# Attention norm of a two-layer decoder step: root and reciprocal on six columns, spread back by TensorE inside the last gate tile

## The chip, the cores and the metric

The kernel runs on one NeuronCore of a Trainium2 chip. The core has TensorE (matrix products, called PE in the rows), VectorE (DVE), ScalarE (ACT), GpSimd (POOL) and SyncE (SP, which issues most loads). The metric is the device time of one execution in microseconds (us); lower is better. Three runs of the kernel before took 2000.6, 2001.98 and 2005.46 us, median 2001.98 us.

## The reference

512 prompt tokens and 32 sample tokens (8 sequences of 4) go through two layers. Each layer is a half SwiGLU, a mixer with two head groups, and another half SwiGLU. The mixer's softmax group has 8 query heads of 64 channels; its output `o_s` (544 tokens by 512 channels) is normalised over the channels of each token, and then goes with the output of the other group (gated linear attention, GLA) through one projection:

```python
def rmsnorm(x, g):
    y = xf * lax.rsqrt(jnp.mean(xf * xf, axis=-1, keepdims=True) + EPS)
    return (y * g.astype(jnp.float32)).astype(x.dtype)

o_s, k_keep, v_keep = swa_fn(qs, ks, vs, sinks)
o_s = rmsnorm(o_s, swa_g)
x = x + jnp.concatenate([o_g, o_s.astype(x.dtype)], axis=-1) @ w_out
x = x + 0.5 * swiglu(rmsnorm(x, n2), ffn2_gu, ffn2_down)
```

## The kernel before

Everything lies with channels on the 128 partitions and the 544 tokens along the free dimension, in two halves of 272. Weights come in chunks of 128x1024 (`w_raw`); ScalarE rounds a chunk to its high part (`w_hi`), GpSimd makes the low part (`w_lo`), and TensorE multiplies three products (high by high, low by high, high by low) for each of eight 128-row pieces. One such weight tile is 48 matmuls of 128x272. A PSUM "pair" is two banks that hold one 128x544 result.

The mixer is one list of steps (`mixer_steps`) that all engines walk through in the same order; each engine does its own part of a step, and semaphores join them. `JOBS` are the projection tiles in that order: job 19 is the gate tile `rG2`, job 20 is `squares` (no weight tile, only the norm's sum), job 21 is the last gate tile `rG3`, and jobs 22 to 29 are `out0` to `out7`, the half of the output projection that reads the normalised softmax output. Behind each job come the steps of its slot. What matters here:

- Slot 17, `ssq`: ScalarE squares the four 128-channel blocks of the attention output `qS`.
- Slot 18, `s_add`: VectorE adds the four blocks of squares into one, `sq_tile(0)` (lines 2274 and 2275).
- Job 20, `squares`: TensorE multiplies this tile by a 128x128 matrix of ones (line 943, two matmuls of 272 columns). Every partition of the pair then holds each token's sum.
- Slot 20: `s_norm` is a root on ScalarE over 128x544 (line 1611) and a reciprocal on VectorE over 128x544 (line 2278). `gs_kv 0` is a state update of the sample tokens, 16 small matmuls (line 1195) and an addition on VectorE (line 2266). `smix 0` and `smix 1` scale `qS` (line 2281); ScalarE then copies the high part (line 1623) and VectorE subtracts for the low part (line 2085).
- Slot 21, behind `rG3`: `att 3` (line 1134 on TensorE, line 2237 on VectorE), `smix 2`, `o 2` (lines 1149, 1155), `kv 6` and `kv 7` (line 1119 on TensorE, line 2222 on VectorE, tile `s_ring`), `smix 3`, and four SiLUs on ScalarE.
- Job 22, `out0`: 24 matmuls in four groups of six; group k waits until part k of the normalised output has its low part (`mix_ready`). It writes the PSUM pair that `squares` used.

In the feed-forward halves a norm over tokens is already done on six columns: `norm_sum` makes sums of one column for pieces of up to 128 tokens (`PIECES`: four of 128, two of 16), ScalarE and VectorE do root and reciprocal on 4 and 2 columns (lines 1285 and 1720), and `norm_spread` brings them to all partitions by six matmuls against the identity (line 797), in the middle of a weight tile.

Of the kernel before, what the change touches and what calls it, by code (L numbers as in the profile page):

```python
# [109 lines left out]


def job_pair(i):

    return 2 if i == 0 else 0 if i == 2 else i % 2
# [19 lines left out]
def mixer_steps():  # L134
# [35 lines left out]
            19: [("att", 2), ("o", 1), ("kv", 4), ("kv", 5)],  # L170
            20: [("s_norm", 0), ("gs_kv", 0), ("smix", 0), ("smix", 1)],
            21: [("att", 3), ("smix", 2), ("o", 2), ("kv", 6), ("kv", 7), ("smix", 3)] +
# [31 lines left out]
def trunk(nc, xT, stream, gains, lparams, wa2, cos_t, sin_t, swa_mask, samp_mask, gla_mask,  # L204
# [5 lines left out]
    def sb(name, shape, dt=F32, at=None):  # L210

        size = int(np.prod(shape[1:])) * 4
        if at is None:
            at = plan["at"]
            plan["at"] += -(-size // 64) * 64
        return nc.alloc_sbuf_tensor_at(name, list(shape), dt, offset=at)

    ctx = ExitStack()
    with ctx:
# [46 lines left out]
        bm = sb("bm", [P, 2])  # L266
        nrt = sb("nrt", [P, len(PIECES)])
        assert plan["at"] <= nc.sbuf_usable_end, plan["at"]
        LG, BG, GG, SG, SK, SKS, LG1 = 0, 24, 26, 30, 34, 42, 44
# [58 lines left out]
        def pair(i):  # L328
            return ps[:, 2 * i:2 * i + 2, 0:TH]

        def halves(ap):
            return ap.rearrange("p (h n) -> p h n", h=2)
# [72 lines left out]
        def sq_tile(j):  # L405
            return (g_buf, sq_buf)[j // 2][:, j % 2, :]

        def go_out():

            return ps[:, 6, 0:4 * SAMP].rearrange("p (h b g t) -> p h b g t", h=2, b=NB, g=2)  # L410
# [6 lines left out]
        def sem(name):  # L417
# [76 lines left out]
                   "ga_out", "go_done", "go_out", "klm_made", "fourfold", "s0_scaled", "gkv_done", "gkv_used", "r_silu",  # L494
                   "gsq", "gss_done", "g_root", "g_recip", "gbc_done", "ssq", "s_added", "ssum_done", "s_root", "q_paired",
                   "mix_made", "mix_high", "mix_ready", "kb_made"]
# [265 lines left out]
        def _(pe):  # L762
# [10 lines left out]

            def model_tile(dst, chunk, slot, h, stage=None, middle=None):

                pe.wait_ge(lo_ready, chunk + 1)
                for k in range(KT):
                    if stage is not None and k >= 5:
                        pe.wait_ge(*h_tile(stage, k))
                    if k == KT // 2 and middle is not None:  # L780
                        norm_spread(middle)
                    ins = product(dst, slot, k * P, h[:, 0, k, :], h[:, 1, k, :], k == 0, k == KT - 1)
                return ins
# [8 lines left out]
            def norm_spread(phase):  # L792

                pe.wait_ge(rs_ready, phase + 1)
                for c, (at, w) in enumerate(PIECES):
                    o = at % TH
                    ins = pe.matmul(ps[:, 6 + at // TH, o:o + w], nrt[0:w, c:c + 1].to_broadcast([w, P]),  # L797
                                    ident[0:w, 0:w], start=True, stop=True)
                ins.then_inc(rs_spread, 1)
# [139 lines left out]

            def square_sum(dst, squares):  # L940

                for hf in range(2):
                    ins = pe.matmul(dst[:, hf, :], ones[:, :], squares[:, hf * TH:(hf + 1) * TH],
                                    start=True, stop=True)
                return ins

            def mixer(l):
                ch = l * PL_LAYER + PL_MIX
                stage = l * 3 + 1
                for pos, (step, i) in enumerate(STEPS):  # L950
                    if step == "in":
# [3 lines left out]
                        if i >= 3:  # L955
                            pe.wait_ge(m["in_used"], i - 1)
                        dst = pair(job_pair(i))
                        if name == "squares":
                            pe.wait_ge(m["s_added"], 1)
                            ins = square_sum(dst, sq_tile(0))  # L960
                            ins.then_inc(m["ssum_done"], 1)
                            continue
                        if name[:3] == "out":
                            output_half(ch, 0, int(name[3]), dst)
                            continue
# [10 lines left out]
                        if name == "a":  # L976
                            for part in range(2):
                                pe.wait_ge(lo_ready, ch + (c + part + 1))
                                for k in range(4 * part, 4 * part + 4):
                                    ins = product(dst, (PL_MIX + c + part) % RING, (k % 4) * P, h_mid[:, 0, k, :],  # L980
                                                  h_mid[:, 1, k, :], k == 0, k == KT - 1)
                                if part == 0:
                                    ins.then_inc(chunk_done, 1)
                        else:
                            ins = model_tile(dst, ch + c, (PL_MIX + c) % RING, h_mid,
                                             stage if i == 0 else None, stage if i == 1 else None)
                        ins.then_inc(chunk_done, 1)
# [238 lines left out]
                for n in range(KT):  # L1226
                    if n == 2:
                        pe.wait_ge(m["in_used"], len(JOBS))
                    if n >= 4:
                        pe.wait_ge(*h_tile(l * 3 + 2, n - 4))  # L1230
                    output_half(ch, 1, n, pair((n + 2) % 4))
# [12 lines left out]
        def _(act):  # L1244
# [239 lines left out]
            def mixer(l):  # L1484
# [9 lines left out]
                for pos, (step, i) in enumerate(STEPS):  # L1494
# [108 lines left out]
                    elif step == "silu":  # L1603
                        act.wait_ge(m["in_used"], JOBS.index(f"rG{i}") + 1)
                        act.activation(rG[:, i, :], rG[:, i, :], ACT.Silu).then_inc(m["r_silu"], 1)
# [3 lines left out]
                    elif step == "s_norm":  # L1609
                        act.wait_ge(m["ssum_done"], 1)  # L1610
                        act.activation(halves(sq_tile(0)), pair(job_pair(JOBS.index("squares"))), ACT.Sqrt,
                                       bias=eps[:, :], scale=1.0 / (4 * P)).then_inc(m["s_root"], 1)
                    elif step == "gss":
# [77 lines left out]
        def _(dve):  # L1691
# [356 lines left out]
            def mixer(l):  # L2048
# [39 lines left out]
                for pos, (step, i) in enumerate(STEPS):  # L2088
# [182 lines left out]
                    elif step == "s_add":  # L2271
# [3 lines left out]
                        dve.tensor_tensor(sq_tile(0), sq_tile(0), sq_tile(3), ALU.add).then_inc(m["s_added"], 1)  # L2275
                    elif step == "s_norm":
                        dve.wait_ge(m["s_root"], 1)
                        dve.reciprocal(sq_tile(0), sq_tile(0)).then_inc(m["in_used"], 1)
                        dve.wait_ge(m["in_used"], JOBS.index("squares") + 1)
                    elif step == "smix":  # L2280
                        dve.scalar_tensor_tensor(out=qS[:, i, :], in0=qS[:, i, :],
                                                 scalar=lp[:, SG + i:SG + i + 1], in1=sq_tile(0),
                                                 op0=ALU.mult, op1=ALU.mult).then_inc(m["mix_made"], 1)
# [19 lines left out]

                dve.wait_ge(m["in_used"], len(JOBS))

# [160 lines left out]
```

## Time and profile before

| | us |
|---|---|
| median of three runs (lowest, highest) | 2001.98 (2000.6, 2005.46) |
| the profiled execution's own time | 1999.98 |
| its span, first to last instruction | 1998.2 |
| TensorE busy | 1951.4 (98%) |
| VectorE busy | 1350.1 (68%) |
| ScalarE busy | 1102.8 (55%) |
| GpSimd busy | 1094.3 (55%) |
| TensorE's mean granted clock, share of full | 0.988 |

The two mixers' stretches around the change are at 545 to 600 us (first layer) and 1525 to 1580 us (second layer) of the span. TensorE is busy nearly all the time, so a VectorE duration counts only where TensorE waits for it. A row of the chain shows which engine the end of the program hangs on at each moment; a row of the timeline gives the start, the duration and, in brackets, the idle time before it and what ended that. A matmul in plain fp32 stands as two records, so six matmuls are "x12".

### The profile page before, as it was taken

What the parts mean: (1) busy time and instruction counts of PE and PEld (TensorE: products, weight loads), DVE (VectorE), ACT (ScalarE), POOL (GpSimd) and SP (SyncE); (2) the same over time, 40 slices, a digit from 0 to 9 for tenths busy, and PEclk for the clock granted to TensorE, in tenths of its full rate; (3) what the DMA queues carried; (4) which work ended last, traced back from release to release, by engine and by line L of the source; (5) the groups of instructions that cost most, each with busy time, mean ns of one, the idle gap of its engine ahead of it and who ended that gap; (6) DMA issues with size and microseconds to landing.
All of it is one profiled execution on the core that took longest, in us unless ns stands there. A gap on an engine that the chain in (4) does not pass through costs nothing.

```text
span 1998.2 us, 40845 instructions
## 1 busy us (share of the span) xinstructions
PE 1951.4 (98%) x15562; PEld 1916.9 (96%) x15562; DVE 1350.1 (68%) x2450; ACT 1102.8 (55%) x2184; POOL 1094.3 (55%) x811
## 2 busy tenths in 40 slices
PE   5999999999999999999999999999999999999997
PEld 5999999998989999999999999999988899999997
DVE  7976687487245886578678757865764559766874
ACT  4664566536234565466656646663542356645662
POOL 3665566732215576566766656675222166755664
PEclk9999999999989999999999999999999999999998
DMA  3233232421211233233323333323121122332231
GB/s 136 82 108 108 85 101 91 150 85 45 94 59 64 78 106 106 93 99 101 99 81 101 101 101 101 105 88 138 64 95 47 67 80 91 100 108 91 96 107 65
DMA packets 92114, 185.65 MB, mean 93 GB/s; under 512 B 12880, under 2 KB 22768, under 8 KB 91376
## 3 DMA queue, kind: packets, MB, share of 16 engines
q1 hardware_dynamic: 84096, 170.04, 25.6%
q10 hardware_dynamic: 7824, 13.00, 1.9%
q8 instruction: 124, 2.03, 0.4%
q14 instruction: 70, 0.57, 0.1%
HBM read 178.09 MB, written 6.95 MB: 93 GB/s over the span
## 4 chain that ended last, share of the span: by engine, by line
PE 93%; DVE 5%; issue 1%; ACT 1%; DMA 0%; POOLq 0%; POOL 0%; DVEq 0%; ACTq 0%
PE ps L809 56%; PE ps L769 23%; PE ps L818 7%; PE ps L1038 1%; PE ps L1155 1%; PE ps L1027 1%; PE ps L1149 1%; PE ps L797 1%; PE ps L1208 1%; PE ps L1221 1%; PE ps L1010 0%; PE ps L1183 0%; DVE h_end L1703 0%; DVE h_end L1700 0%; PE ps L789 0%
## 5 line engine op out<-in xcount | busy, mean ns | idle before, releaser
L809 PE MATMUL ps<-rhs,w_hi 128*128 128x272 f32 x4256 | 805.0, 288 | 0.0
L809 PEld LDWEIGHTS ps<-rhs,w_hi 128*128 128x128 f32 x4256 | 669.6, 188 | 0.6 <-DVE ssum L1890 0.6
L809 PE MATMUL ps<-rhs,w_lo 128*128 128x272 f32 x2128 | 613.9, 288 | 0.0
L646 POOL TENSOR_TENSOR w_lo<-w_raw,w_hi 128x512 fp32r<-128x512 f32 x272 | 351.3, 1297 | 252.0 <-ACT w_hi L1308 252.0
L640 POOL TENSOR_TENSOR w_lo<-w_raw,w_hi 128x1024 fp32r<-128x1024 f32 x80 | 191.1, 2390 | 404.9 <-ACT w_hi L1252 390.4
L809 PEld LDWEIGHTS ps<-rhs,w_lo 128*128 128x128 f32 x2128 | 402.3, 189 | 0.0
L809 PE MATMUL ps<-act_c,w_hi 128*128 128x272 f32 x1792 | 354.5, 289 | 1.1 <-DVE h_mid L1741 0.8
L646 POOL TENSOR_TENSOR w_lo<-s_tmp,w_hi 128x512 fp32r<-128x512 f32 x216 | 283.1, 1323 | 32.6 <-ACT w_hi L1308 32.3
L809 PEld LDWEIGHTS ps<-act_c,w_hi 128*128 128x128 f32 x1792 | 287.7, 188 | 1.8 <-DVE h_mid L1741 1.2
L769 PE MATMUL ps<-h_mid,w_hi 128*128 128x272 f32 x1600 | 278.3, 292 | 0.0
L809 PE MATMUL ps<-act_c,w_lo 128*128 128x272 f32 x896 | 258.3, 288 | 0.0
L769 PEld LDWEIGHTS ps<-h_mid,w_hi 128*128 128x128 f32 x1600 | 229.4, 190 | 3.4 <-issue 2.8
L1308 ACT ACTIVATE w_hi<-ps 128x512 fp32r<-128x512 f32 x216 | 129.4, 599 | 182.1 <-DVE ps L1766 171.2
L1308 ACT ACTIVATE w_hi<-w_raw 128x512 fp32r<-128x512 f32 x272 | 172.1, 633 | 47.4 <-PE ps L809 40.3
L1308 ACT ACTIVATE w_hi<-s_tmp 128x512 fp32r<-128x512 f32 x216 | 136.7, 633 | 87.3 <-PE ps L809 86.0
L809 PEld LDWEIGHTS ps<-act_c,w_lo 128*128 128x128 f32 x896 | 169.3, 189 | 0.0
L769 PE MATMUL ps<-h_mid,w_lo 128*128 128x272 f32 x800 | 166.2, 289 | 0.0
L1766 DVE TENSOR_TENSOR s_tmp<-ps,w_raw 128x512 f32<-128x512 f32 x216 | 148.4, 687 | 17.4 <-POOL w_lo L646 3.1
L818 PE MATMUL ps<-act_p,pl_hi 128*128 128x272 f32 x768 | 159.5, 287 | 0.0
L1766 DVE TENSOR_TENSOR ps<-ps,w_raw 128x512 f32<-128x512 f32 x216 | 149.6, 692 | 2.7 <-ACT ps L1359 0.7
L1252 ACT ACTIVATE w_hi<-w_raw 128x1024 fp32r<-128x1024 f32 x76 | 80.2, 1058 | 127.9 <-PE ps L769 117.1
L1772 DVE TENSOR_TENSOR w_lo<-ps,w_hi 128x512 fp32r<-128x512 f32 x216 | 141.3, 683 | 1.2
(292 smaller groups left out, 3260.0 us busy)
## 6 DMA issues: line engine op xcount, KB each, us to landing
w_raw<-stream SPq DMA_DIRECT2D x380, 256.0 KB, 2.9
w_raw<-stream SPq DMA_DIRECT2D x80, 512.0 KB, 3.2
g_buf<-stream SPq DMA_DIRECT2D x52, 256.0 KB, 2.8
pl_raw<-stream SPq DMA_DIRECT2D x64, 192.0 KB, 2.8
x<-xT ACTq DMA_DIRECT2D x8, 272.0 KB, 5.7
y_d<-x SPq DMA_DIRECT2D x8, 272.0 KB, 2.1
s<-s_d ACTq DMA_DIRECT2D x2, 1024.0 KB, 4.9
s_s_d<-s ACTq DMA_DIRECT2D x2, 1024.0 KB, 3.9
```

Source lines behind the costliest of these rows:

```text
L640: pool.tensor_tensor(w_lo[:, p % RING, :], w_raw[:, p % RAW, :], w_hi[:, p % RING, :].bitcast(F32), ALU.subtract).then_inc(lo_ready, 1)
L646: pool.tensor_tensor(operand(w_lo, j, half), source(op, s, half), operand(w_hi, j, half).bitcast(F32), ALU.subtract).then_inc(pool_low, 1)
L769: ins = pe.matmul(dst[:, hf, :], w[:, slot, cols], r[:, hf * TH:(hf + 1) * TH], start=first and w is w_hi and r is rhs_hi, stop=last and r ...
L797: ins = pe.matmul(ps[:, 6 + at // TH, o:o + w], nrt[0:w, c:c + 1].to_broadcast([w, P]), ident[0:w, 0:w], start=True, stop=True)
L809: ins = pe.matmul(bank(s, at), w[:, k * P:(k + 1) * P], moving[:, k, side, r, :], start=fresh and k == 0 and w is hi and side == 0, stop=k ...
L818: ins = pe.matmul(bank(s, at), w[:, k * P:(k + 1) * P], act_p[:, k, side, hf * TH:(hf + 1) * TH], start=False, stop=k == PLAIN - 1 and sid ...
L1027: ins = pe.transpose(ps[:, 6 + a // 2, o:o + WIN], s_tile(i)[:, a * 256 + kb * WIN:a * 256 + (kb + 1) * WIN], ident[:, :])
L1038: ins = pe.matmul(ps[g * HD:(g + 1) * HD, 6, uu * WIN:(uu + 1) * WIN], vs_tok[:, b - 1 + kb, g * HD:(g + 1) * HD], p_t[:, o:o + WIN], star ...
L1252: act.activation(w_hi[:, p % RING, :], w_raw[:, p % RAW, :], ACT.Copy).then_inc(hi_ready, 1)
L1308: act.activation(operand(w_hi, j, half), source(op, s, half), ACT.Copy).then_inc(op_high, 1)
L1766: dve.tensor_tensor(source(name, s, half), first, second, ALU.add).then_inc(sum_made, 1)
L1772: dve.tensor_tensor(operand(w_lo, j, half), source(op, s, half), operand(w_hi, j, half).bitcast(F32), ALU.subtract).then_inc(dve_low, 1)
```

## The change

The sum over channels, the root and the reciprocal are done by tokens. `squares` on TensorE becomes six matmuls with one moving column: the stationary operand is a piece of the summed squares, and the result is one PSUM column per piece. ScalarE takes the root of 4 and 2 columns into a new small tile `sst`; VectorE takes the reciprocal there. TensorE spreads them to all partitions in six matmuls against the identity, placed in the middle of the weight tile `rG3`, into the same PSUM pair. The four `smix` steps read their factor from PSUM rather than from SBUF. The reciprocal's step moves behind `gs_kv 0` on VectorE, where VectorE then also waits for the spread. Since the pair is read until `smix 3`, `out0` on TensorE now waits for all four `smix` steps. The summed squares no longer count as an evacuated job (`evacuated`).

```diff
+def evacuated(i):
+    return i - (i > JOBS.index("squares"))
-            20: [("s_norm", 0), ("gs_kv", 0), ("smix", 0), ("smix", 1)],
+            20: [("s_norm", 0), ("gs_kv", 0), ("s_recip", 0), ("smix", 0), ("smix", 1)],
+        sst = sb("sst", [P, len(PIECES)])
+        def squares():
+            return pair(job_pair(JOBS.index("squares")))
...
+                    if k == KT // 2 and inside is not None:
+                        inside()
...
-            def square_sum(dst, squares):
-                for hf in range(2):
-                    ins = pe.matmul(dst[:, hf, :], ones[:, :], squares[:, hf * TH:(hf + 1) * TH],
-                                    start=True, stop=True)
-                return ins
+            def square_spread():
+                pe.wait_ge(m["s_recip"], 2)
+                for c, (at, w) in enumerate(PIECES):
+                    ins = pe.matmul(squares()[:, at // TH, at % TH:at % TH + w], sst[0:w, c:c + 1].to_broadcast([w, P]),
+                                    ident[0:w, 0:w], start=True, stop=True)
+                ins.then_inc(m["s_spread"], 1)
...
-                            ins = square_sum(dst, sq_tile(0))
+                            for c, (at, w) in enumerate(PIECES):
+                                ins = pe.matmul(dst[0:w, 0, c:c + 1], sq_tile(0)[:, at:at + w], ones[:, 0:1],
+                                                start=True, stop=True)
...
                         if name[:3] == "out":
+                            if name == "out0":
+                                pe.wait_ge(m["mix_made"], 4)
...
-                                             stage if i == 0 else None, stage if i == 1 else None)
+                                             stage if i == 0 else None, stage if i == 1 else None,
+                                             square_spread if name == "rG3" else None)
...
-                        act.activation(halves(sq_tile(0)), pair(job_pair(JOBS.index("squares"))), ACT.Sqrt,
-                                       bias=eps[:, :], scale=1.0 / (4 * P)).then_inc(m["s_root"], 1)
+                        w = PIECES[-1][1]
+                        act.activation(sst[:, 0:4], squares()[:, 0, 0:4], ACT.Sqrt, bias=eps[:, :],
+                                       scale=1.0 / (4 * P)).then_inc(m["s_root"], 1)
+                        act.activation(sst[0:w, 4:6], squares()[0:w, 0, 4:6], ACT.Sqrt, bias=eps[0:w, :],
+                                       scale=1.0 / (4 * P)).then_inc(m["s_root"], 1)
...
-                    elif step == "s_norm":
-                        dve.wait_ge(m["s_root"], 1)
-                        dve.reciprocal(sq_tile(0), sq_tile(0)).then_inc(m["in_used"], 1)
-                        dve.wait_ge(m["in_used"], JOBS.index("squares") + 1)
+                    elif step == "s_recip":
+                        dve.wait_ge(m["s_root"], 2)
+                        w = PIECES[-1][1]
+                        dve.reciprocal(sst[:, 0:4], sst[:, 0:4]).then_inc(m["s_recip"], 1)
+                        dve.reciprocal(sst[0:w, 4:6], sst[0:w, 4:6]).then_inc(m["s_recip"], 1)
+                        dve.wait_ge(m["s_spread"], 1)
                     elif step == "smix":
-                        dve.scalar_tensor_tensor(out=qS[:, i, :], in0=qS[:, i, :],
-                                                 scalar=lp[:, SG + i:SG + i + 1], in1=sq_tile(0),
+                        dve.scalar_tensor_tensor(out=halves(qS[:, i, :]), in0=halves(qS[:, i, :]),
+                                                 scalar=lp[:, SG + i:SG + i + 1], in1=squares(),
```

The first place is TensorE's order from job 20 to the end of `rG3`. Before, it is the two wide sums, the 16 matmuls of `gs_kv` and an unbroken weight tile; line 769 is the weight tile's product.

```order
L1119 MATMUL ps<-v_tok,klT 64x128 x8
L943 MATMUL ps<-g_buf,ones 128x272 x2
L1195 MATMUL ps<-v_tok,klm 64x128 x16
L769 MATMUL ps<-h_mid,w_hi 128x272 x2
L769 MATMUL ps<-h_mid,w_lo 128x272 x2
```

Now, with line 779 for the same product, the one-column sums stand in the place of the wide ones, and the six spreading matmuls stand where the fifth of the tile's eight pieces begins.

```order
L974 MATMUL ps<-ones,g_buf 128x1 x4
L974 MATMUL ps<-ones,g_buf 16x1 x2
L1213 MATMUL ps<-v_tok,klm 64x128 x16
...
L779 MATMUL ps<-h_mid,w_hi 128x272 x2
L956 MATMUL ps<-ident,sst 128x128 x4
L956 MATMUL ps<-ident,sst 128x16 x2
L779 MATMUL ps<-h_mid,w_hi 128x272 x2
```

So TensorE's queue has eight more matmuls in each layer, and six of them lie inside a weight tile.

The second place is VectorE's order in slots 20 and 21. Before:

```order
L2222 SCALAR_TENSOR_TENSOR s_ring<-s_ring,ebl,ps 128x128 x4
L2278 RECIPROCAL g_buf<-g_buf 128x544
L2266 TENSOR_TENSOR s_110<-ps,s_110 128x1024
L2281 SCALAR_TENSOR_TENSOR qS<-qS,lp,g_buf 128x544 x2
L2085 TENSOR_TENSOR mixS_lo<-qS,mixS_hi 128x544
L2124 TENSOR_TENSOR rG<-ps,rs 128x544
L2237 COPY_PREDICATED attm<-m_gla,ps 128x256 x2
L2281 SCALAR_TENSOR_TENSOR qS<-qS,lp,g_buf 128x544
```

Now, in the changed kernel's line numbers:

```order
L2243 SCALAR_TENSOR_TENSOR s_ring<-s_ring,ebl,ps 128x128 x4
L2287 TENSOR_TENSOR s_111<-ps,s_111 128x1024
L2300 RECIPROCAL sst<-sst 128x4
L2301 RECIPROCAL sst<-sst 16x2
L2304 SCALAR_TENSOR_TENSOR qS<-qS,lp,ps 128x544 x2
L2106 TENSOR_TENSOR mixS_lo<-qS,mixS_hi 128x544
L2145 TENSOR_TENSOR rG<-ps,rs 128x544
L2258 COPY_PREDICATED attm<-m_gla,ps 128x256 x2
```

The wide reciprocal is gone, the state update comes first, and the two small reciprocals follow it; the rest keeps its order.

The third place is the start of `out0` on TensorE, with what each instruction waits for. Before:

```order
L1119 MATMUL ps<-v_tok,klT 64x128 [waits m_att_out]
L1119 MATMUL ps<-v_tok,klT 64x128 x3
L769 MATMUL ps<-mixS_hi,w_hi 128x272 [waits m_mix_ready,lo_ready,m_in_used]
L769 MATMUL ps<-mixS_hi,w_hi 128x272
L769 MATMUL ps<-mixS_hi,w_lo 128x272 x2
```

Now:

```order
L1137 MATMUL ps<-v_tok,klT 64x128 [waits m_att_out]
L1137 MATMUL ps<-v_tok,klT 64x128 x3
L779 MATMUL ps<-mixS_hi,w_hi 128x272 [waits lo_ready,m_mix_ready,m_mix_made,m_in_used]
L779 MATMUL ps<-mixS_hi,w_hi 128x272
L779 MATMUL ps<-mixS_hi,w_lo 128x272 x2
```

The first matmul of `out0` has one more semaphore to wait for, `m_mix_made`, which here stands for the fourth `smix`.

## Rows read from the trace of the kernel before

**Rows 1.** The page, the chain that ended last, by engine.

```profile
PE 93%; DVE 5%; issue 1%; ACT 1%; DMA 0%; POOLq 0%; POOL 0%; DVEq 0%; ACTq 0%
```

**Rows 2.** TensorE's waits, 1538 to 1557 us: us in total, times, longest.

```profile
PE ps L769 <- DVE mixS_lo L2085: 1.0, 1, 1.0
PE ps L1195 <- DVE s_ring L2222: 0.5, 1, 0.5
```

**Rows 3.** Chain in order of time, second layer: start us, us, what.

```profile
1540.82 6.22 PE ps L769 x48
...
1551.70 0.61 PE ps L1119 x16
...
1553.68 0.70 DVE qS L2281
1554.38 0.65 DVE mixS_lo L2085
...
1555.07 1.84 PE ps L769 x12
```

**Rows 4.** The same view, first layer: `out0`, `out1` and `out2`.

```profile
573.60 4.54 PE ps L769 x24
...
581.96 3.21 PE ps L769 x24
...
593.24 4.84 PE ps L769 x24
```

**Rows 5.** TensorE's timeline at the mixer's own norm, 391 to 398 us.

```profile
391.75 1.13 PE L789 MATMUL ps<-ones,ssum 128*128 128x1 f32 x12
...
395.67 0.41 PE L769 MATMUL ps<-h_mid,w_hi 128*128 128x272 f32 x2
395.92 1.59 PE L797 MATMUL ps<-ident,nrt 128*128 128x128 f32 x12
397.45 0.52 PE L769 MATMUL ps<-h_mid,w_hi 128*128 128x272 f32 x2
397.80 0.41 PE L769 MATMUL ps<-h_mid,w_lo 128*128 128x272 f32 x2
```

**Rows 6.** TensorE's timeline, first layer, from the sums to the middle of `rG3`.

```profile
559.47 1.18 PE L943 MATMUL ps<-g_buf,ones 128*128 128x272 f32 x4
561.16 0.70 PE L1195 MATMUL ps<-v_tok,klm 32*64 32x128 f32 x32 [0.51 <-DVE s_ring L2222]
...
564.66 0.67 PE L769 MATMUL ps<-h_mid,w_hi 128*128 128x272 f32 x4
```

**Rows 7.** VectorE's timeline, first layer, slots 20 and 21.

```profile
561.68 3.55 DVE L2278 RECIPROCAL g_buf<-g_buf 128x544 f32<-128x544 f32 x1 [0.78 <-ACT g_buf L1611]
565.27 1.22 DVE L2266 TENSOR_TENSOR s<-ps,s 128x1024 f32<-128x1024 f32 x1
566.41 1.47 DVE L2281 SCALAR_TENSOR_TENSOR qS<-qS,lp,g_buf 128x544 f32<-128x544 f32 x2
...
569.85 2.67 DVE L2281 SCALAR_TENSOR_TENSOR qS<-qS,lp,g_buf 128x544 f32<-128x544 f32 x1
```

**Rows 8.** GpSimd's timeline, 563 to 580 us, its only row.

```profile
569.60 2.35 POOL L640 TENSOR_TENSOR w_lo<-w_raw,w_hi 128x1024 fp32r<-128x1024 f32 x1 [11.75 <-ACT w_hi L1252]
```

**Rows 9.** ScalarE's and VectorE's timelines at the mixer's own norm.

```profile
393.08 0.24 ACT L1286 ACTIVATE nrt<-ps,eps 16x2 f32<-16x2 f32 x1
...
393.42 0.18 DVE L1720 RECIPROCAL nrt<-nrt 128x4 f32<-128x4 f32 x1 [2.81 <-ACT nrt L1286]
```

**Rows 10.** Stretches: length, busy of each engine, then the granted clock (PEclk), DMA, GB/s.

```profile
568.01:572.66 4.65, 4.65 (x33) 3.78 (x32) 4.65 (x6) 1.61 (x3) 2.35 (x1) 1.00 0.00 0
572.66:576.40 3.74, 3.74 (x29) 3.38 (x29) 3.09 (x8) 1.82 (x5) 0.00 (x0) 0.54 0.42 140
...
1552.24:1555.07 2.83, 1.78 (x17) 1.56 (x13) 2.54 (x6) 1.14 (x3) 0.00 (x0) 1.00 0.47 174
...
1571.33:1576.73 5.40, 5.40 (x26) 5.40 (x25) 0.28 (x2) 0.41 (x2) 0.00 (x0) 0.52 0.55 222
```

More of the change, by code:

```diff
@@ L494, in trunk @@
                    "ga_out", "go_done", "go_out", "klm_made", "fourfold", "s0_scaled", "gkv_done", "gkv_used", "r_silu",
-                   "gsq", "gss_done", "g_root", "g_recip", "gbc_done", "ssq", "s_added", "ssum_done", "s_root", "q_paired",
+                   "gsq", "gss_done", "g_root", "g_recip", "gbc_done", "ssq", "s_added", "ssum_done", "s_root", "s_recip", "s_spread", "q_paired",
                    "mix_made", "mix_high", "mix_ready", "kb_made"]
@@ L772, in product, with model_tile @@
                 return ins
-            def model_tile(dst, chunk, slot, h, stage=None, middle=None):
+            def model_tile(dst, chunk, slot, h, stage=None, middle=None, inside=None):
                 pe.wait_ge(lo_ready, chunk + 1)
@@ L955, in mixer @@
                         if i >= 3:
-                            pe.wait_ge(m["in_used"], i - 1)
+                            pe.wait_ge(m["in_used"], evacuated(i - 1))
                         dst = pair(job_pair(i))
@@ L1227, in mixer @@
                     if n == 2:
-                        pe.wait_ge(m["in_used"], len(JOBS))
+                        pe.wait_ge(m["in_used"], evacuated(len(JOBS)))
                     if n >= 4:
@@ L1603, in mixer @@
                     elif step == "silu":
-                        act.wait_ge(m["in_used"], JOBS.index(f"rG{i}") + 1)
+                        act.wait_ge(m["in_used"], evacuated(JOBS.index(f"rG{i}") + 1))
                         act.activation(rG[:, i, :], rG[:, i, :], ACT.Silu).then_inc(m["r_silu"], 1)
@@ L2301, in mixer @@
                             low_part(7, a_buf[:, i % 2, :])
-                dve.wait_ge(m["in_used"], len(JOBS))
+                dve.wait_ge(m["in_used"], evacuated(len(JOBS)))
                 def evacuate(n):
```

## The prediction, made before the changed kernel ran

> **What bounds the kernel now.** I read the page first. The chain that ended last runs on TensorE for 93% of the span and on VectorE for 5% [rows 1]. So a microsecond taken from VectorE or ScalarE counts only where TensorE stands still for it, and a microsecond added to TensorE's queue counts in full unless it falls into such a standstill. Next I read TensorE's waits around the change. In the second layer there are two: 0.5 us before the state update's matmuls, on `s_ring`, and 1.0 us inside `out0`, on the low part of the third block of the normalised output [rows 2]. Then the chain there: the gate tile `rG3` (6.22 us), the small matmuls to the end of `kv 7` at 1552.31, four `s_ring` updates, the fourth `smix` from 1553.68 to 1554.38, one low part to 1555.02, and the second half of `out0` at 1555.07 [rows 3]. The wide reciprocal is not in that chain. It takes 3.55 us of VectorE [rows 7], but in the time of `rG3`. In the first layer TensorE has no wait in `out0`: it runs its 24 matmuls in 4.54 us, where `out1` takes 3.21 [rows 4], because the granted clock fell to its lower level, 1.2 GHz, for the first half of it [rows 10].
>
> **The sums.** The two wide sums go. In the first layer they start at 559.47 and take 1.18 us, to 560.65; then TensorE stands 0.51 us, because the state update's matmuls wait for `s_ring` and start only at 561.16 [rows 6]. Six one-column sums of the mixer's own norm take 1.13 us [rows 5], so they would end at 560.60, and the next matmul still starts at 561.16. Cost and gain: 0. What hides it is the wait for `s_ring`; without it the difference would be the 0.05 us. Bounds: -0.1 to +0.1 us.
>
> **Root and reciprocal.** Two small roots replace the wide one, two small reciprocals the wide one. The small ones take 0.24 us and 0.18 us [rows 9]. VectorE now does the state addition first: its matmuls end at 561.16 + 0.70 = 561.86, the addition takes 1.22 us [rows 6, 7], to about 563.1, and the two reciprocals end by 563.5. TensorE wants them at the fifth piece of `rG3`, which starts 0.25 us into the row at 564.66, so at 564.91 [rows 6]. That leaves 1.4 us, so the new wait on `s_recip` costs nothing. If that cover went, each microsecond would be TensorE's. Behind the wait stands the second half of `rG3`, for which VectorE, ScalarE and GpSimd all wait in turn.
>
> **The spread.** Six matmuls against the identity go into `rG3`, with nothing to hide them. At the mixer's own norm the same six stand between two products of a weight tile: products are 0.25 us apart (395.67 to 395.92), the spread takes from 395.92 to 397.45, 1.53 us, and the products behind it are 0.35 apart once, 0.10 more than usual [rows 5]. So +1.63 us per layer, +3.3 us for two. Bounds: 1.4 (the busy time of the sums and a little, as if the wide sums' time were partly given back) to 1.9 us per layer.
>
> **The scaling.** VectorE waits for the spread, which ends at about 566.5. Before, it started `smix 0` at 566.41 [rows 7]. So the first two `smix` steps come at the same time as before and are over before `rG3` ends, which is now 1.63 us later. The third `smix` took 2.67 us at 569.85, where half of the row of two took 0.74 [rows 7]; it overlaps GpSimd's subtraction of 569.60 to 571.95 [rows 8]. With its factor in PSUM it may be 1.9 us shorter. VectorE then waits longer for `kv 6`, which TensorE computes behind `o 2`; that end is set by TensorE. So the 1.9 us and the 3.4 us of reciprocal are VectorE's own and I count both at 0. The Trainium skill says that GpSimd's SBUF interfaces are shared with VectorE and that instructions with two SBUF inputs contend ("GPSIMD Engine Reference", section 1). By that rule the third `smix` loses its stall for good; the sum stays the same either way, since TensorE does not stand for it.
>
> **The wait before `out0`.** Now `out0` may not start before the fourth `smix` is made. That `smix` ends at 1554.38, 2.07 us after TensorE's last `kv` matmul at 1552.31 [rows 3]; this distance is made of VectorE's `s_ring` updates and the `smix`, and neither gets shorter. Before, `out0` did its first 12 matmuls in that time and stood for the third group. Now the whole of it comes behind: its length is that of `out1`, 3.21 us [rows 4], and a start from a standstill costs 0.24 more (12 matmuls in 1.84 instead of 1.60 us [rows 3, 4]). With 0.04 from `smix` to matmul it ends at 1554.42 + 3.45 = 1557.87 instead of 1555.07 + 1.84 = 1556.91: +0.96 us. In the first layer: 573.60 + 2.07 + 0.04 + 3.45 = 579.16 instead of 573.60 + 4.54 = 578.14 [rows 4]: +1.02. Together +2.0 us. Bounds: 0.7 us per layer (no start cost) to 2.1 (the whole wait, if the parts behind were late too). Queued behind the waiting matmul are `o 3`, `out1` and the GLA norm, so all other engines shift with it. TensorE's other waits up to the feed-forward half are for work that TensorE itself feeds, so nothing gives the time back.
>
> **The clock.** This is the term with no row of its own. The granted clock is at the full 2.4 GHz through the small matmuls from 568.01 to 572.66 and at half right behind them, with no standstill. Behind the one-column sums of the GLA norm it is low in both layers: the 24 matmuls of `out2` take 5.40 us there (second layer, clock 0.52) and 4.84 us (first) instead of 3.21 [rows 4, 10]. So one fall that lands on a weight product costs 1.6 to 2.2 us. The change makes such falls likelier: it takes wide columns out in front of `rG3` and puts a standstill of 2.1 us between the small matmuls and `out0`. In the first layer a fall is there already and costs nearly nothing, because `out0` stood for VectorE anyway; now it would count. Bounds: 0 to four falls (two places, two layers), 8 us. I take one, 1.9 us, the middle of the two rows. The Trainium skill puts it that the throttled state is the default and activity releases it ("TensorE: Matmul & The Clock Gate", part 1). By that rule alone both layers would fall in the new standstill, +3.8 us; but the stretch of the second layer with the 1.0 us standstill ran at the full clock [rows 10], so the trace bears it out only in part.
>
> **Sum.** 0 + 3.3 + 2.0 + 1.9 = +7.2 us. Against the profiled execution's own time that is 1999.98 + 7.2 = 2007.2 us (span 1998.2 + 7.2 = 2005.4). The median of the runs shown is 2.0 us above that execution, so as a median I forecast 2001.98 + 7.2 = 2009.2 us.
>
> **The rivals.**
> 1. *No new fall.* The two certain terms alone: +5.3 us, 2007.3 us. For it: the second layer's `out0` ran at the full clock through a standstill of 1.0 us [rows 2, 10]. Against it: the standstill is now twice as long.
> 2. *A fall in each layer*, on `out0` or on `rG3`: 5.3 + 2 x 1.9 = +9.1 us, 2011.1 us; with a third one 2013. For it: both layers ran `out2` at the lower clock behind the GLA norm's sums [rows 4, 10]. Against it: `out0` of the second layer, as in rival 1.
> 3. *The wait before `out0` is hidden anyway.* If the fourth `smix` is early, since VectorE has 5.3 us less to do, only the spread is left: +3.3 us, 2005.3 us. Against it: the chain shows the fourth `smix` directly behind the `s_ring` updates, and these behind TensorE's `kv` [rows 3].
> 4. *Faster.* The reciprocal does set the end: its 3.55 us less 0.3, and the 1.9 us of the third `smix`, come off the path in each layer, against 1.63 + 1.0 added: -2.5 us per layer, -5.0, 1997.0 us. It decides only if TensorE stands for the scaling by more than the 2.6 us added; the rows have 1.0 us in one layer and none in the other, so more would have to be hidden in what the rows call busy.
>
> **How the numbers follow.** Forecast (one fall) 0.36, rival 1 0.27, rival 2 0.20, rival 3 0.11, rival 4 0.06. What a measurement here can tell from no change is about 0.3%, 6.0 us. The forecast's 7.2 lies close above it, so I count three quarters of it (0.27), all of rival 2 (0.20) and a quarter of rival 1 (0.07) as slower: 0.54. Faster is rival 4, 0.06. The rest, 0.40, is within 0.3%. The range leaves out rival 4 and the far end of rival 2: 2004 to 2013 us.
>
> **What would show it.** Right: `rG3` in the chain at about 7.8 us instead of 6.2, with about 1.5 us of spread inside and no wait in front of it; TensorE standing about 2.1 us before `out0`, released by `smix`; the third `smix` at about 0.8 us; VectorE busy some 10 us less in all; and somewhere between `squares` and `out1` a stretch at half clock that covers wide products. Wrong: a wait of TensorE on `s_recip`, an `out0` that starts without waiting, or a TensorE that is not later at `out1` than before by 2.6 us per layer at equal clock. A time below 2002 us would say that the reciprocal counted after all.

## The result: 0.76% slower, twice what was forecast

| us | before | changed |
|---|---|---|
| median (lowest, highest), 4 runs each | 2001.94 (2000.6, 2005.46) | 2017.2 (2013.85, 2022.49) |
| profiled execution, own time | 1999.98 | 2013.85 |
| its span | 1998.2 | 2012.0 |
| mean granted clock of TensorE | 0.988 | 0.983 |

The ratio is 1.0076, 95% interval [1.0051, 1.0101]: +15.2 us (10 to 20). The forecast was 2009.2 us with a range of 2004 to 2013. The direction was right; the size was not, and the time lies outside the range. The difference is small, under 1%, but the interval lies well clear of zero.

### The profile page after: what moved, and what is told of

It is laid out like the page before. It is cut to its first block, busy times and chain, and to the rows that moved or that the text cites. A ratio compares the mean times of both kernels' runs of the same rounds, so it can differ in the third digit from the quotient of the medians.

```text
span 2012.0 us, 40931 instructions
## 1 busy us (share of the span) xinstructions
PE 1963.0 (98%) x15602; PEld 1929.4 (96%) x15602; DVE 1343.2 (67%) x2452; ACT 1102.0 (55%) x2186; POOL 1093.4 (54%) x811
## 3 DMA queue, kind: packets, MB, share of 16 engines
q8 instruction: 125, 2.05, 0.4%
## 4 chain that ended last, share of the span: by engine, by line
PE 93%; DVE 4%; issue 1%; ACT 1%; DMA 0%; POOLq 0%; POOL 0%; ACTq 0%; DVEq 0%
PE ps L821 55%; PE ps L779 23%; PE ps L830 7%; PE ps L1056 1%; PE ps L1173 1%; PE ps L1045 1%; PE ps L1167 1%; PE ps L1226 1%; PE ps L809 1%; PE ps L1239 1%; PE ps L1028 0%; DVE h_end L1721 0%; PE ps L801 0%; PE ps L1201 0%; DVE st L2088 0%
## 5 line engine op out<-in xcount | busy, mean ns | idle before, releaser
L779 PE MATMUL ps<-h_mid,w_hi 128*128 128x272 f32 x1600 | 282.6, 295 | 0.0
```

Of the source, the lines that this page charges most:

```text
L779: ins = pe.matmul(dst[:, hf, :], w[:, slot, cols], r[:, hf * TH:(hf + 1) * TH], start=first and w is w_hi and r is rhs_hi, stop=last and r ...
```

## The profile after

The page shows the same chain, and VectorE with less work, as forecast (1350.1 us before, with the 93% of [rows 1]):

```profile
PE 1963.0 (98%) x15602; PEld 1929.4 (96%) x15602; DVE 1343.2 (67%) x2452; ACT 1102.0 (55%) x2186; POOL 1093.4 (54%) x811
...
PE 93%; DVE 4%; issue 1%; ACT 1%; DMA 0%; POOLq 0%; POOL 0%; ACTq 0%; DVEq 0%
```

The chain in order of time (start us, us, what), first layer of the changed kernel. Line 974 is the one-column sums, 1213 the state update's matmuls, 956 the spread, 779 the weight tiles, 1137 `kv`, 1226 the GLA norm's sums:

```profile
558.16 1.85 PE ps L974 x12
560.00 1.08 PE ps L1213 x32
561.09 5.02 PE ps L779 x24
566.11 1.43 PE ps L956 x12
567.55 3.20 PE ps L779 x24
...
575.40 1.07 PE ps L1137 x16
576.48 2.16 issue
578.63 4.83 PE ps L779 x24
...
587.28 3.21 PE ps L779 x24
...
592.65 5.48 PE ps L1226 x40
598.13 5.26 PE ps L779 x24
```

Against [rows 3, 4]: `rG3` was one block of 48 matmuls in 6.22 us and is now two halves with the spread between them. The second half takes 3.20 us, the first 5.02. The chain calls the 2.16 us in front of 578.63 "issue" and names no releaser. That they are the new wait is read from VectorE's timeline, where the fourth `smix` ends at 578.53:

```profile
577.76 0.77 DVE L2304 SCALAR_TENSOR_TENSOR qS<-qS,lp,ps 128x544 f32<-128x544 f32 x1
```

`out0` behind the wait takes 4.83 us, where `out1` takes 3.21. The second layer has the same picture:

```profile
1545.38 1.16 PE ps L1213 x32
1546.54 5.47 PE ps L779 x24
1552.02 1.43 PE ps L956 x12
1553.45 3.22 PE ps L779 x24
...
1561.94 2.16 issue
1564.09 4.78 PE ps L779 x24
...
1578.06 7.28 PE ps L1226 x40
1585.34 4.92 PE ps L779 x24
```

The stretches of the changed kernel say why the long pieces are long. First layer (stretch, length, busy of PE, PEld, DVE, ACT, POOL, then granted clock, DMA share, GB/s):

```profile
558.09:561.02 2.93, 2.93 (x49) 2.57 (x45) 1.21 (x4) 1.83 (x4) 0.00 (x0) 0.53 0.34 138
561.02:570.67 9.65, 9.65 (x68) 9.36 (x60) 3.54 (x6) 1.32 (x2) 0.00 (x0) 0.79 0.01 2
...
575.33:578.63 3.30, 1.15 (x17) 0.77 (x17) 2.00 (x6) 0.72 (x3) 0.00 (x0) 0.50 0.46 159
578.63:583.30 4.67, 4.67 (x24) 4.67 (x25) 1.27 (x2) 4.17 (x6) 0.00 (x0) 0.62 0.00 0
583.30:603.23 19.93, 18.38 (x147) 17.15 (x146) 2.95 (x5) 5.71 (x10) 2.35 (x1) 0.83 0.22 86
```

Three stretches of its second layer (sums with state update, `kv` with the standstill, `out0`):

```profile
1543.69:1546.47 2.78, 2.32 (x48) 1.92 (x45) 1.21 (x4) 1.83 (x4) 0.00 (x0) 0.69 0.32 131
...
1561.26:1564.09 2.83, 0.68 (x17) 0.46 (x17) 2.00 (x6) 0.72 (x3) 0.00 (x0) 1.00 0.51 181
1564.09:1568.71 4.62, 4.62 (x25) 4.62 (x26) 1.26 (x2) 4.17 (x6) 0.00 (x0) 0.63 0.01 4
```

The same pieces in the kernel before, first layer: sums with state update, `rG3`, `out0`, then what lies behind:

```profile
559.47:561.79 2.32, 1.81 (x41) 1.16 (x37) 1.32 (x5) 2.15 (x3) 0.00 (x0) 1.00 0.45 178
561.79:568.01 6.22, 6.22 (x56) 6.08 (x49) 6.16 (x5) 0.75 (x2) 0.00 (x0) 1.00 0.01 3
...
573.53:577.99 4.46, 4.46 (x29) 4.43 (x26) 3.27 (x7) 2.53 (x4) 0.00 (x0) 0.68 0.23 83
577.99:597.92 19.93, 18.38 (x147) 17.15 (x145) 2.95 (x5) 7.65 (x14) 2.35 (x1) 0.83 0.22 86
```

The clock column is the reading. In the first layer sums and state update ran at 1.00 before and run at 0.53 now, that is, nearly all the time at the lower level of 1.2 GHz; `rG3` went from 1.00 to 0.79.

The column also says when the clock fell. In the first layer it was down before the standstill began: `kv` (575.40) takes 1.07 us instead of 0.61, and its stretch stands at 0.50. The kernel before had such a fall at the same `kv` (0.87 us in its chain, 0.54 in [rows 10]); there the clock was back before `out0` ended, while now `out0` is slow for most of its length. In the second layer the clock was full through the standstill and fell on `out0`.

From the sums to the end of `out2`, the first layer grew from 38.45 us (559.47 to 597.92) to 45.14 (558.09 to 603.23), the second from 38.30 (1538.43 to 1576.73) to 46.40 (1543.69 to 1590.09): +14.8 us, against 13.8 in the whole span; the rest of the program is 1.0 us shorter. What lies behind `out0` in the first layer is equally long, 19.93 us both times.

The forecast gave 5.3 us of these 14.8 to the spread and the wait. The other 9.5 us lie in stretches at the lower clock.

## The experiments

All times are against the kernel before on the same chip; each kernel ran 5 to 12 times, and one of these executions was traced. A measurement is given as the ratio of the times with its 95% interval, and then as the difference in us. "Clock theory" is: each part of the change provokes a fall of TensorE's granted clock to its lower level at its own place, and that makes the missing time. The rival: the falls are chance or come from the shift of the program, or the missing time lies in one part's direct price.

**One line alone: `out0` waits (e1_out0_wait).**

```diff
+                            if name == "out0":
+                                pe.wait_ge(m["mix_made"], 4)
```

> The kernel before, with one line of the change alone: out0 waits for the fourth smix. Clock theory (the missing 8 us are falls of the granted clock that each part of the change provokes at its own place): 2.0 us for the two waits, and a fall of the clock on out0 behind the standstill of 2.1 us in each layer, 1.5 to 2 us each: +5 to +6 us. Rival (the falls are chance, or belong to the shift of the whole program): +2.0 us, and no new stretch at half clock on out0.

Measured: 1.0038 [1.0022, 1.0054], +7.6 us (4.4 to 10.8). More than the rival's 2.0, and the clock theory's 5 to 6 lie inside. The chain of its first layer:

```profile
559.61 2.03 PE ps L943 x4
561.64 1.08 PE ps L1197 x32
...
574.08 1.07 PE ps L1121 x16
575.15 2.17 issue
577.31 4.51 PE ps L769 x24
...
585.64 3.21 PE ps L769 x24
```

The wait is as long as in the changed kernel, and `out0` behind it is slow (in the second layer 5.54 us). But this execution also has a fall that the edit can't have made: the two wide sums (line 943) and the state update in front of it are as in the kernel before, and take 2.03 and 1.08 us instead of 1.18 and 0.70 [rows 6]. The clock is back for `rG3`. So falls come without the change too; how often, is counted at the end of this section.

**The narrow sums alone (e2_narrow_sums).** Six one-column sums for the two wide ones; nothing reads them.

```diff
-                            ins = square_sum(dst, sq_tile(0))
+                            for c, (at, w) in enumerate(PIECES):
+                                ins = pe.matmul(dst[0:w, 0, c:c + 1], sq_tile(0)[:, at:at + w], ones[:, 0:1],
+                                                start=True, stop=True)
...
-                        act.activation(halves(sq_tile(0)), pair(job_pair(JOBS.index("squares"))), ACT.Sqrt,
+                        act.activation(sq_tile(0), sq_tile(0), ACT.Sqrt,
```

> The kernel before, with the six one-column sums in place of the two wide ones and nothing else moved. The root reads the summed squares in SBUF instead of their sums, so that the softmax output is not normalised by the right factor. Clock theory: the wide columns in front of the state update kept the clock up; without them it falls there in both layers and half of rG3 runs at 1.2 GHz: +2.4 us per layer, +4 to +5 us. Rival: the one-column sums are hidden behind the wait for s_ring and the clock stays: 0 us.

Measured: 1.0024 [1.0014, 1.0035], +4.8 us (2.8 to 7.0), as the clock theory said. Its chain in the first layer (the sums are line 961):

```profile
559.76 1.68 PE ps L961 x12
561.44 1.11 PE ps L1197 x32
562.55 8.18 PE ps L769 x48
```

`rG3`, which this experiment doesn't change, takes 8.18 us instead of 6.22 [rows 3], and 8.39 in the second layer.

**The spread alone (e3_spread_alone).**

```diff
+                pe.wait_ge(m["s_root"], 1)
+                for c, (at, w) in enumerate(PIECES):
+                    pe.matmul(pair(0)[:, at // TH, at % TH:at % TH + w], nrt[0:w, c:c + 1].to_broadcast([w, P]),
+                              ident[0:w, 0:w], start=True, stop=True)
...
+                                             extra_spread if name == "rG3" else None)
```

> The kernel before, with six spreading matmuls added in the middle of rG3 (they spread the factors of the layer's first norm into the free PSUM pair, which nothing reads). Both theories: 1.63 us per layer, +3.3 us. Clock theory: no new fall, since the spread stands between wide columns. A rival that puts the missing time on the spread itself: +8 us or more.

Measured: 1.0020 [1.0011, 1.0029], +4.0 us (2.2 to 5.8), with 3.3 inside. (One more execution took 4849.74 us, with a cause that isn't known; it isn't in the ratio.) The spread has its priced size, and `rG3` around it is at full speed:

```profile
560.53 3.22 PE ps L769 x24
563.74 1.43 PE ps L946 x12
565.18 3.19 PE ps L769 x24
...
574.35 5.57 PE ps L769 x24
```

The `out0` at 574.35 ran at the lower clock here, without any new wait in front of it (5.25 us in the second layer). So 7.6 + 4.8 + 4.0 = 16.4 us for the three parts apart, and 15.2 for them together.

**The wait, but not idle (e5_wait_filled).** As e1, with 16 matmuls of 128x272 in the standstill.

```diff
+                                pe.wait_ge(m["in_used"], JOBS.index("rG3") + 1)
+                                for k in range(16):
+                                    pe.matmul(pair(1)[:, k % 2, :], h_mid[:, 0, k % 8, 0:P], h_mid[:, 1, k % 8, 0:TH],
+                                              start=True, stop=True)
                                 pe.wait_ge(m["mix_made"], 4)
```

> The kernel before with out0's wait for the fourth smix (as in e1_out0_wait), and 16 matmuls of 128x272 put into the standstill, whose results nothing reads: about 2.0 us of wide columns where TensorE would stand 2.1 us. The path is as long as in e1. Clock theory (e1's time above 2.0 us is a fall of the clock behind the idle standstill): out0 at the full clock in both layers, +2 to +2.5 us against before, 3 us or so less than e1. Rival (the time is in the wait itself, or the clock falls for the small matmuls ahead of it whatever follows): as e1, +5.7 us.

Measured: 1.0003 [0.9990, 1.0017], +0.6 us (-2.0 to +3.4). The same wait on the same path, 7 us less than e1. So e1's time is for the most part not in waiting but in waiting idle. That is more than e1's two slow `out0` account for: over the forecast's 3.45 us they lost 1.1 and 2.1 us. The profiled execution, at 2010.86 us one of the two slowest of twelve (median 2002.83), shows that a fall can still come:

```profile
575.72 3.92 PE ps L967 x16
579.64 3.50 PE ps L769 x24
```

`kv` is slow before the filling begins (1.07 us), as in e1. The clock stays down on the filling matmuls (line 967; 3.92 us, in the second layer 3.02, where 16 at full speed take about 2.1, by `rG3`'s 6.22 us for 48), and `out0` takes 3.50 and 3.01 us. So in this execution the filling did not prevent the fall; it took it in place of `out0`. What the faster executions did wasn't traced.

**The changed kernel without `out0`'s wait for `smix` (e6_after_copied).**

```diff
-                                pe.wait_ge(m["mix_made"], 4)
+                                pe.wait_ge(m["s_copied"], 1)
...
+                    elif step == "s_recip":
+                        act.wait_ge(m["s_spread"], 1)
+                        act.activation(halves(sq_tile(0)), squares(), ACT.Copy).then_inc(m["s_copied"], 1)
...
-                        dve.scalar_tensor_tensor(out=halves(qS[:, i, :]), in0=halves(qS[:, i, :]),
-                                                 scalar=lp[:, SG + i:SG + i + 1], in1=squares(),
+                        dve.scalar_tensor_tensor(out=qS[:, i, :], in0=qS[:, i, :],
+                                                 scalar=lp[:, SG + i:SG + i + 1], in1=sq_tile(0),
```

> The changed kernel, but ScalarE copies the spread factor from PSUM to SBUF (128x544) and the smix steps read it there, so that out0 waits for the copy alone and not for the fourth smix. Clock theory: out0's standstill of 2.1 us and the fall behind it go; what is left is the spread (+3.3) and the fall in front of rG3 (+4.5): +8 to +9 us against before, about 6 us less than the changed kernel's 15. Rival (the falls have nothing to do with the standstill): only the 2.0 us of the wait come back, +13 us.

Measured: 1.0040 [1.0026, 1.0053], +8.0 us (5.2 to 10.6), as the clock theory said; 13 lies outside. In its trace `out0` is at full speed in both layers, and the first half of `rG3` is slow in both (4.06 and 5.50 us).

**The changed kernel with 128 columns per sum (e7_after_wide_sums).**

```diff
-                                ins = pe.matmul(dst[0:w, 0, c:c + 1], sq_tile(0)[:, at:at + w], ones[:, 0:1],
+                                ins = pe.matmul(ps[0:w, c // 4, c % 4 * WS:(c % 4 + 1) * WS],
+                                                sq_tile(0)[:, at:at + w], ones[:, 0:WS],
...
```

> The changed kernel, but each of the six sums streams 128 columns of ones instead of one (the same sum stands in 128 columns, the root reads one of them). The six take about 1.5 us instead of 1.1, just under what the wait for s_ring hides. Clock theory: these columns keep the clock up in front of rG3 as the wide sums did: 4 to 5 us less than the changed kernel, +10 us against before. Rival (the fall there comes from the missing columns only by chance of position, or from the state update): no less than the changed kernel, +15 us.

Measured: 1.0049 [1.0036, 1.0062], +9.8 us (7.2 to 12.4), as forecast; the rival's 15 lies outside. The interval overlaps that of the changed kernel (10 to 20), so this run alone doesn't show how much came back. And the trace differs from what I had expected. First layer:

```profile
558.38 2.79 PE ps L975 x12
...
561.79 3.19 PE ps L780 x24
...
566.42 3.22 PE ps L780 x24
```

`rG3` is at full speed, but the sums are slow, 2.79 us (2.97 in the second layer), where e8's same sums take 1.63: the clock fell before them and was back in front of the weight tile. In this execution the fall moved onto cheaper work rather than going away. The expectation had said that the columns keep the clock up; the traces show only that the clock is back sooner.

**Everything mended, and the GLA norm too (e8_after_three, e4_gla_sums_wide).** e4 is the kernel before with the 20 one-column sums of the GLA norm made 96 columns wide; e8 is the changed kernel with e6's copy, e7's sums, and this.

```diff
-                                ins = pe.matmul(ps[0:w, 4, c:c + 1], sq_tile(h)[:, tb * P:tb * P + w],
-                                                ones[:, 0:1], start=True, stop=True)
+                                ins = pe.matmul(ps[0:w, 4 + h, tb * WG:(tb + 1) * WG], sq_tile(h)[:, tb * P:tb * P + w],
+                                                ones[:, 0:WG], start=True, stop=True)
...
```

> The kernel before, with the one-column sums of the GLA norm (20 per layer) made 96 columns wide: the same sums stand in 96 columns. Clock theory: idle columns are what lets the clock fall there, so the fall behind them goes in most executions: each sum costs at most 0.03 us more per record and 1 us per layer, and the 24 matmuls of out2 take 3.2 instead of 4.8 to 5.4 us, the later sums are at full clock too: -2 to -4 us over both layers. Rival (the standstill of 1.55 us in front of them is enough to bring the clock down, or the falls are chance): 0 to +2 us.

> The changed kernel with all three: factor copied to SBUF, 128-column sums, and the GLA norm's sums 96 columns wide (as in e4_gla_sums_wide). Clock theory: spread +3.3, no fall from the change left, and e4's gain of about 4 to 5 us: -2 to 0 us against before. So the time by tokens would not beat e4 alone, since the spread has no cover. Rival (falls by chance): +8 us or more.

Measured: e4 0.9979 [0.9967, 0.9990], -4.2 us (-6.6 to -2.0). e8 1.0003 [0.9994, 1.0012], +0.6 us (-1.2 to +2.4), a shade above its forecast. The chain of e4 in the first layer, where [rows 4] had 4.84 us for the `out2` at 593.24:

```profile
585.63 5.42 PE ps L1208 x40
591.05 3.20 PE ps L770 x24
```

and its clock in these two stretches:

```profile
585.63:591.05 5.42, 5.42 (x41) 4.47 (x41) 0.00 (x0) 0.28 (x1) 1.41 (x1) 1.00 0.27 97
591.05:594.25 3.20, 3.20 (x26) 3.20 (x27) 0.28 (x2) 0.41 (x2) 0.00 (x0) 1.00 0.71 287
```

The 96-column sums take 5.42 us in both layers, where the one-column ones took 5.91 and 5.30 us in the kernel before, in part at the lower clock. The gain is in `out2` behind them: 3.20 us in both layers instead of 4.84 and 5.50.

**Repeated, and with the last standstill filled (e10_gla_wide_again, e9_gla_filled).**

```diff
+                        for k in range(12):
+                            pe.matmul(pair(0)[:, k % 2, :], h_mid[:, 0, k % 8, 0:P], h_mid[:, 1, k % 8, 0:TH],
+                                      start=True, stop=True)
                         pe.wait_ge(m["gsq"], GH)
```

> The kernel before with the 96-column GLA sums of e4_gla_sums_wide, and 12 matmuls of 128x272 (results unread) in TensorE's standstill of 1.55 us in front of them. Clock theory: that standstill is the last place behind the gates where e4's clock can still fall, so another 0 to 2 us: -4 to -6 us against before. Rival (the columns of the sums did it all, or the filling matmuls are in the way): the same as e4, -4 us, or up to 1 us more.

> e4_gla_sums_wide once more, on the same chip as e9: both theories say about -4 us against before, as in the first runs (-0.21%).

Measured: e10 0.9986 [0.9974, 0.9999], -2.8 us (-5.2 to -0.2); e9 0.9969 [0.9958, 0.9981], -6.2 us (-8.4 to -3.8). Both beat the kernel before. That the filling itself adds to e4 is not shown, as the intervals of e9 and e10 overlap.

**The places counted over all twelve traces.** Each trace holds both layers, so each kernel shows every place twice.

- `rG3`: with one-column sums in front (changed kernel, e2, e6) it was slow in 6 places of 6, by 0.9 to 2.4 us. With wide sums of either kind (the nine others) it was never slow by more than 0.3 us.
- The sums and the state update: with the two wide sums of the kernel before they ran at the lower clock in 7 places of 14, with one-column sums in 6 of 6.
- `out0`: behind the idle wait (changed kernel, e1, e7) slow in 6 places of 6; without any added wait slow in 7 of 16, the first layer of the kernel before among them.
- `out2`: behind one-column GLA sums slow in 16 places of 16 (4.76 to 5.74 us), behind 96-column sums in none of 8 (3.20 or 3.21 us).

So the rival had a part of the truth: falls come without the change, in about half of the places. What narrow sums and an idle wait do is that the low clock is there every time and reaches the weight products.

## Why the prediction was wrong

- **The sums.** (TensorE's queue has ten more matmuls per layer, twelve for two, and not eight as the section on the change says; the page counts 15602 records instead of 15562, which is 40 more: two for each matmul, in two layers.) "Cost and gain: 0" was right for their direct price and wrong as a result, because a stretch priced from a row at the full clock was run at half of it. In the first layer sums and state update took 2.93 us instead of 2.32. e2 puts the whole effect of the narrow sums at 4.8 us.
- **Root and reciprocal.** Right. In the first layer the small reciprocals came at 562.41, behind the state addition, and TensorE's list of waits has none for them.
- **The spread.** Right: 1.43 us in the chain of each layer, +4.0 us alone where 3.3 was forecast.
- **The scaling.** The third `smix` lost its stall, 0.78 us instead of 2.67 [rows 7]. VectorE's timeline after, first layer, with GpSimd's `w_lo` subtraction from 571.98 to 574.33 beside it:

```profile
572.17 0.78 DVE L2304 SCALAR_TENSOR_TENSOR qS<-qS,lp,ps 128x544 f32<-128x544 f32 x1
572.87 2.05 DVE L2106 TENSOR_TENSOR mixS_lo<-qS,mixS_hi 128x544 fp32r<-128x544 f32 x1
```

  What I said of it, "loses its stall for good", holds for that instruction, but the next one reads both inputs from SBUF and now takes 2.05 us instead of 0.71 (in both layers). So the trace agrees with the rule of the Trainium skill ("GPSIMD Engine Reference", section 1) on both instructions, and VectorE saved 6.9 us in all instead of the 10 that I named. None of it was on the path.
- **The wait before `out0`.** Right in place and length (2.16 us in both layers). Its direct price of 2.0 us fits too: from the end of `kv` to the end of `out0` the layers grew by 2.45 and 2.33 us, and less what `out0` lost to the clock that is 1.1 and 1.0. e5's 0.6 us (up to 3.4) allows it.
- **The clock. This is the step that failed:** "I take one, 1.9 us, the middle of the two rows." Weight products ran slow in all four places, the first half of `rG3` and `out0`, in both layers. In the traces it was so in every place with narrow sums or an idle wait, 12 of 12: not a draw of one in four. One of the four stood in the prediction's own text, "In the first layer a fall is there already", and was then not counted apart. I gave the bound myself, "0 to four falls (two places, two layers), 8 us", and cut it off in the range. The price of one, 1.9 us, was about right: the first halves of `rG3` took 1.9 and 2.4 us more than the 3.1 of half a tile at full clock, the two `out0` 1.4 and 1.3 us more than the 3.45 I had worked out. That is 7.0 of the 9.5 us. The slow small matmuls around them are another 1.1 us (0.61 and 0.46 us over the 2.32 us), and the second layer's GLA norm, in a longer low stretch than before, is the last 1.4 us, by 21.38 us against 19.99.
- **The rule that I weighed against the trace.** The Trainium skill says that the throttled state is the default and activity releases it ("TensorE: Matmul & The Clock Gate", part 1). I took the second layer's 1.0 us standstill without a fall as evidence against it and gave the case of a fall in each layer 0.20. The trace now agrees with the rule: `out0` is slow in both layers, though in the first the clock was down before the standstill. The evidence against it was thin: one execution, with one standstill of half the length in the middle of `out0`. The same untouched `out0` of the second layer took 5.53 us in e9's trace.
- **Rivals.** 1 (no new fall), 3 (the wait is hidden) and 4 (faster) fell. Rival 2 was the right mechanism, with two falls of the four: 9.1 of the 15.2 us.

What stays open: why a particular execution has a particular fall, and why narrow sums and an idle wait bring it on; the runs show that they do. The four runs of the changed kernel, at mean clocks 0.983, 0.981, 0.981 and 0.979, took 2013.85, 2017.15, 2017.26 and 2022.49 us, so runs with more time at the lower clock are longer, and the profiled one was the best of them.

## What to carry to other kernels

Before replacing a wide matmul by a narrow one, or adding a wait on the engine that sets the end, look at the granted clock of the stretches around it and price the next wide products at the lower clock too; if the same kernel already shows slow products behind similar work, count every such place, not one of several. A place at full clock in one trace is weak evidence, since the same place can be slow in the next execution. Cheap columns can be worth having: 96 instead of 1 in the GLA norm's sums made the kernel faster by 0.14 to 0.21% with the same number of instructions. And work taken off an engine that is not waited for gives nothing, here 6.9 us of VectorE, while six small matmuls in TensorE's queue cost their full length (1.43 us per layer in the trace).

## What the runs showed of the hardware beyond what I expected

- A busy TensorE can lose its clock: in the changed kernel the stretch 558.09 to 561.02 is 2.93 us of 2.93 busy and ran at 0.53, and the 1.50 us of small matmuls before 557.50 were as busy, at 1.00. The busy share doesn't tell the two apart.
- Filling a standstill of 2.1 us with 16 matmuls whose results nobody reads took e1's +7.6 us down to +0.6 us, though in the one traced execution the clock was low on the filling.
- VectorE's stall beside a GpSimd `tensor_tensor` isn't bound to an instruction but to the overlap: take one out of its way and the next with two SBUF inputs stalls (0.71 to 2.05 us, in both layers).
